# Decoder step on one core: two more feed-forward tiles by seven block products, sums moved between early tiles, and a regrouped norm of the last tokens

## What is computed

```python
x = x + g1 * rmsnorm(mixed, p['norm_post_mix'])
h2 = rmsnorm(x, p['norm_pre_ffn']) * (1 + sc2) + sh2
fg, fu = jnp.split(h2 @ p['w_ffn_in'], 2, axis=-1)        # 1024 -> 2 x 2816
ff = (jax.nn.silu(fg) * fu) @ p['w_ffn_out']              # 2816 -> 1024
x = x + g2 * rmsnorm(ff, p['norm_post_ffn'])
```

## Time and profile before

| | us |
|---|---|
| time, median of 3 runs (lowest to highest) | 1398.78 (1397.47 to 1404.78) |
| profiled execution: its time | 1403.48 |
| its span, first to last instruction | 1401.7 |
| PE busy in the span | 1352.4 (96%) |
| mean granted TensorE clock | 0.985 |

### The profile page before, as it was taken

How to read it: one execution, slowest core, us unless ns; L and a number is a source line. 1 busy time by engine, 2 the same in 40 slices (tenths; PEclk the granted TensorE clock), 3 DMA queues, 4 the chain that set the end, 5 groups by cost and what they waited for, 6 DMA issues and landing times.

```text
span 1401.7 us, 24171 instructions
## 1 busy us (share of the span) xinstructions
PE 1352.4 (96%) x10132; PEld 1256.8 (90%) x10132; DVE 793.5 (57%) x1110; ACT 555.8 (40%) x815; POOL 211.6 (15%) x320
## 2 busy tenths in 40 slices
PE   6899999999999999999999999999889999999996
PEld 3799999988997898799889978999789999999995
DVE  4459888522252484267437624874866788853224
ACT  4477778211222321232214123336543566542221
POOL 1122232000123222302320222000001111100001
PEclk8999999999999999999999999999999999999998
DMA  9422222582525334424442443336024676743323
GB/s 366 151 76 91 61 76 79 220 334 97 189 65 190 114 109 156 163 93 136 151 157 78 138 163 121 91 93 228 33 78 113 166 187 163 175 134 100 93 83 64
DMA packets 60267, 188.30 MB, mean 134 GB/s; under 512 B 6528, under 2 KB 9728, under 8 KB 59776
## 3 DMA queue, kind: packets, MB, share of 16 engines
q1 hardware_dynamic: 44096, 141.28, 29.7%
q0 software_dynamic: 14912, 43.39, 11.8%
q10 hardware_dynamic: 1152, 2.10, 0.4%
HBM read 163.19 MB, written 23.55 MB: 133 GB/s over the span
## 4 chain that ended last, share of the span: by engine, by line
PE 84%; DVE 9%; ACT 3%; issue 2%; DMA 1%; POOL 0%; SPq 0%; DVEq 0%; ACTq 0%; POOLq 0%
PE ps L893 56%; PE ps L1294 12%; PE ps L902 3%; PE ps L1142 2%; PE ps L1153 2%; PE ps L945 1%; PE ps L1125 1%; PE ps L1185 1%; PE ps L1171 1%; PE ps L1028 1%; DVE w_lo L1781 1%; ACT w_hi L1369 1%; PE ps L1082 1%; PE ps L1095 0%; DVE hs L1898 0%
## 5 line engine op out<-in xcount | busy, mean ns | idle before, releaser
L893 PE MATMUL ps<-h_hi,w_hi 128*128 128x272 f32 x1584 | 336.7, 294 | 7.6 <-DVE h_lo L1800 5.8
L893 PE MATMUL ps<-h_hi,w_lo 128*128 128x272 f32 x1584 | 329.6, 290 | 0.0
L893 PE MATMUL ps<-h_lo,w_hi 128*128 128x272 f32 x1584 | 328.6, 289 | 0.0
L1781 DVE TENSOR_TENSOR w_lo<-raw,w_hi 128x1024 fp32r<-128x1024 f32 (+2 forms) x158 | 187.1, 1188 | 218.3 <-ACT w_hi L1369 216.4
L893 PEld LDWEIGHTS ps<-h_hi,w_hi 128*128 128x128 f32 x1584 | 252.4, 190 | 20.9 <-issue 12.2
L1369 ACT ACTIVATE w_hi<-raw 128x1024 fp32r<-128x1024 f32 (+2 forms) x158 | 161.8, 1025 | 255.7 <-PE ps L893 150.3
L893 PEld LDWEIGHTS ps<-h_lo,w_hi 128*128 128x128 f32 x1584 | 250.8, 190 | 0.0
L893 PEld LDWEIGHTS ps<-h_hi,w_lo 128*128 128x128 f32 x1584 | 249.4, 190 | 0.0
L2058 DVE SCALAR_TENSOR_TENSOR state<-state,ps 128x512 f32<-128x512 f32 x64 | 41.1, 683 | 108.4 <-PE ps L1185 108.2
L2446 POOL DMA_DIRECT2D s_raw<-in_w_fin x16 | 13.8, 866 | 337.0 <-DMA s_raw<-in_w_fin 337.0
L893 PE MATMUL ps<-a_hi,w_hi 128*128 128x272 f32 x308 | 63.8, 288 | 0.3 <-DVE w_lo L1781 0.3
(11 more groups left out here) (291 smaller groups left out, 2634.3 us busy)
## 6 DMA issues: line engine op xcount, KB each, us to landing
raw<-in_w_head SPq DMA_DIRECT2D x48, 512.0 KB, 3.8
state<-in_state POOLq DMA_DIRECT2D x32, 512.0 KB, 4.5
out_rs<-state POOLq DMA_DIRECT2D x32, 512.0 KB, 4.5
raw<-in_w_rnn SPq DMA_DIRECT2D x24, 512.0 KB, 3.6
ada_more<-in_w_ada SPq DMA_DIRECT2D x23, 512.0 KB, 8.2
raw<-in_w_fin SPq DMA_DIRECT2D x22, 512.0 KB, 4.7
ada_raw<-in_w_ada SPq DMA_DIRECT2D x16, 512.0 KB, 14.8
raw<-in_w_bret SPq DMA_DIRECT2D x16, 512.0 KB, 3.5
```

The lines of the kernel that those rows point to most:

```text
L893: mm = nc.tensor.matmul(dst[:, half, :], a, b[:, half * HALF:(half + 1) * HALF], start=first and j == 0, stop=last and j == 2)
L1781: V.tensor_tensor(lo[:, 0:cols], raw_slab(i)[0][:, 0:cols], hi[:, 0:cols].bitcast(F32), ALU.subtract).then_inc(lo_ready, 1)
```

## The change

`FIRST` goes from 6 to 4: only n = 3 is a plain tile, 18 instead of 16 n's are made by block products. The sums of h2 and their splits move from the plain tiles to between the `product_half`s of the second early half. In `second_input(1)` the samples' operations move behind the second scaled tile, one of them ahead of the reciprocal; `silu_half(1, 0)` goes ahead of the root. For the first pair, DVE multiplies the last plain tile before it splits the third weight slab. At the end, PE adds the last tile's squares in PSUM (two matmuls with the ones) instead of DVE's addition; the samples are normed together with the last 160 prompt tokens, in three pieces of 3, 3 and 2 channel tiles, each stored by one DMA; the sum of squares of the first part stands after 4 blocks instead of 8 of the second part; and ACT takes a root of one element after the first output tile.

```diff
-FIRST = 6
+LAST_TILES = (slice(0, 3), slice(3, 6), slice(6, KD))
+FIRST = 4
...
-            for k in range(KD):
-                sp.wait_ge(y_done, k + 1)
-                sp.dma_start(out["y"][:, k, cols], xr_[:, k, cols]).then_inc(stored, 16)
+            for i, ks in enumerate(LAST_TILES):
+                sp.wait_ge(y_done, i + 1)
+                sp.dma_start(out["y"][:, ks, cols], xr_[:, ks, cols]).then_inc(stored, 16)
...
+                        if half and (i, j) == (0, 3):
+                            total_part(("post2", 0), LAST_PARTS[0], 3)
-                    if half and i == 0:
-                        total_part(("post2", 0), LAST_PARTS[0], 3)
-            total_part(("post2", 1), LAST_PARTS[1], 4)
+            pe.wait_ge(sq_added, 2 * KD - 2)
+            nc.tensor.matmul(dst, ccol("ones"), rsn[:, cols], start=True, stop=False)
+            pe.wait_ge(sq_ready, SQUARES)
+            nc.tensor.matmul(dst, ccol("ones"), sqn[:, (KD - 1) % 2, cols], start=False, stop=True).then_inc(full, 1)
...
+            silu_half(1, 0)
             std(("pre2",), 1, rsn, D, eps_rms)
-            silu_half(1, 0)
...
-            ahead(("fg", EARLY))
-            for n in range(EARLY):
-                silu_half(n, 1)
-            keep(1)
+            plain_ahead(("fg", EARLY))
+            silu_half(0, 1)
+            keep(1)
+            act.wait_ge(x1_stored, 16)
+            hi_of_sum(0)
+            hi_of_sum(1)
+            silu_half(1, 1)
+            hi_of_sum(2)
+            hi_of_sum(3)
+            silu_half(2, 1)
...
+                if m == 0:
+                    do(A(sqn[:, 1, 0:1], eps_rms[:, 0:1], ACT.Sqrt), wait=False)
...
+            hs2 = mo[:, :, SEQ:T]
+            do(V.tensor_tensor(all_samples(mo), all_samples(xr_), for_samples(scale2), ALU.mult))
+            product_half(1, 0)
             one_over("pre2", 1)
-            product_half(1, 0)
-            second_input(1)
+            second_input(1, samples_of_second)
...
+            plain_ahead(("fg", EARLY))
+            product_half(0, 1)
+            sums_of_input()
+            product_half(1, 1)
+            lo_of_sum(0)
+            lo_of_sum(1)
+            product_half(2, 1)
+            lo_of_sum(2)
+            lo_of_sum(3)
...
-            add_to_norm(first + KD + 1, KD - 1, LAST_PARTS[1], norm_summed)
             wait_took(dve, ("fo", KD - 1))
+            do(V.tensor_tensor(all_samples(mo), all_samples(mo), for_samples(gate2), ALU.mult))
             dve.wait_ge(xres_in, 32)
             one_over_last(1)
-            samples_normed(gate2)
-            for k in range(KD):
-                add_last(k)
+            for ks in LAST_TILES:
+                add_last(ks)
```

More of the change, by code:

```diff
@@ L1673, in _, with hi_of_sum @@
             silu_half(2, 0)
-            ahead(("fg", EARLY))
-            for n in range(EARLY):
-                silu_half(n, 1)
-            keep(1)
             def plain_ahead(key):
                 split_to(min(pl.slab[(*key, "w", 0)] + AHEAD, last_plain))
+            def hi_of_sum(i):
+                act.wait_ge(x_summed, i + 1)
+                name = ("XC", "XB", "XA", "XD")[i]
+                do(A(x_block(None, x_hi, name), x_block(None, mo, name), ACT.Copy), x_hi_ready, wait=False)
+            plain_ahead(("fg", EARLY))
[8 more added lines that the diff above has]
+            silu_half(2, 1)
             def hi_of_blocks(p, slab):
@@ L1720, in _ @@
                 plain_ahead(("fg", n))
[L1721 to L1725, removed]
                 act.wait_ge(a_ready, EARLY + n - 1 if n >= EARLY + 2 else n + 2)
@@ L2145, in samples_normed, with second_input @@
                 do(V.tensor_tensor(x, x, y, ALU.add))
-            def second_input(half):
+            def second_input(half, between=None):
                 at = prompt_of(half)
@@ L2153, in second_input @@
                                                   ALU.mult), h_scaled, wait=False)
+                    if between is not None and k == 1:
+                        between()
                     if k:
@@ L2191, in _, with samples_of_second @@
                     product_half(0, 0)
+            hs2 = mo[:, :, SEQ:T]
+            do(V.tensor_tensor(all_samples(mo), all_samples(xr_), for_samples(scale2), ALU.mult))
+            product_half(1, 0)
             one_over("pre2", 1)
-            product_half(1, 0)
[L2194 to L2199, removed]
-            second_input(1)
+            def samples_of_second():
+                do(V.tensor_tensor(hs2, hs2, rsn[:, SEQ:T].unsqueeze(1).to_broadcast([P, KD, NS]), ALU.mult))
+                do(V.tensor_tensor(all_samples(mo), all_samples(mo), for_samples(mod[:, 3 * KD:4 * KD, :]), ALU.add))
+                do(V.tensor_copy(h_hi[:, :, SEQ:T], hs2))
+                do(V.tensor_tensor(h_lo[:, :, SEQ:T], hs2, h_hi[:, :, SEQ:T].bitcast(F32), ALU.subtract))
+            second_input(1, samples_of_second)
             product_half(2, 0)
-            ahead(("fg", EARLY))
-            for n in range(EARLY):
-                product_half(n, 1)
             def plain_ahead(key):
@@ L2286, in _ @@
                     gated_pair(p - 1)
-                else:
-                    plain_gated(FIRST - 1)
                 lo_of_blocks(p, 3)
@@ L2291, in _ @@
                     lo_of_gated(p - 1)
+                else:
+                    plain_split(FIRST - 1)
                 if p + 1 < PAIRS:
@@ L2309, in norm_first, with add_last @@
                 do(V.tensor_tensor(y, y, rsn[:, LAST_PARTS[0]], ALU.mult), y_normed, wait=False)
[L2311 to L2313 removed]
+            def add_last(ks):
+                at = LAST_PARTS[1]
+                y, x = mo[:, ks, at], xr_[:, ks, at]
+                r = rsn[:, at].unsqueeze(1).to_broadcast([P, ks.stop - ks.start, at.stop - at.start])
                 do(V.tensor_tensor(y, y, r, ALU.mult))
```

39 lines of the change are left out of this document (23 added, 16 removed).

## The result

The changed kernel takes **1390.25 us** (median of 7 runs, 1389.64 to 1395.01) beside 1398.78 of the kernel before (7 runs, 1397.11 to 1404.78). The ratio is 0.9936, with a 95% interval from 0.9917 to 0.9955: 9.0 us faster, between 6.3 and 11.6. The forecast was 1388.0, with a range of 1384.5 to 1393.0.

A forecast was written before the change was run, and what follows sets the result against it. PE, busy 1352.4 of 1401.7 us, was taken to bound the kernel, with the end behind its last matmul. Terms of 3.0, 3.2, 2.8 and 1.8 sum to 10.8 us, off the median 1398.78: 1388.0 us, range 1384.5 to 1393.0.

The forecast's parts named there:

- two more tiles by products: Feed-forward input: two n's by block products save 24 matmuls of 0.125 us, 3.0 us, if a pair stays PE's.
- first pair: First block pair: product ahead of third slab's split removes PE's 1.8 us wait and a slow stretch of 1.4; 3.2 us.
- second early half: Second early half: first `h_lo` 1.8 us earlier, 1.0 us wait for `product_half(0, 1)` gone; 2.8 us, bounds 1.0 and 3.2.
- the end: Program's end: accumulations start 1.3 us earlier, stores without holes give 0.5; 1.8 us, bounds nothing and 3.6.
- holes between the stores: Program's end: DVE's late data left gaps among the last stores; their removal counted as 0.5 us.
- the two queues run side by side: Program's end: stores' packets should lie behind the accumulations'; stores and accumulations side by side would prove the prediction wrong.
- just fits: Second early half: product of `(2, 0)` frees its banks at 1029.2, PE asks at 1029.3, so no wait.
- The stores land on their own: Rival, program's end: accumulations don't hold stores back, gain there 3.6 us instead of 1.8, 1386.2 us; chance 0.08.
- The sums come late: Rival, second early half: `keep`, sums or splits 2.5 us later, 2 to 4 us less gain, 1391 us; chance 0.14.
- the first pair still waits: Rival, first block pair: PE waits for the third slab instead, 3.2 us less gain, 1391.2 us; chance 0.08.
- A pair stayed PE's: Block pairs: DVE's 8.5 us fit in PE's 10.5; rival that DVE sets the pace, 1406 us, chance 0.03.
- the third slab: Second early half: weight slab whose late load delayed `product_half(0, 1)`; no longer asked for there, 1.0 us.

The follow-up runs named there:

- e6: Changed kernel with FIRST = 6, and only two slabs of the plain tiles split ahead of the second half's first gate; 1393.17 us, 0.9958 of before.
- t2: Changed kernel with POOL's four last DMAs as plain writes, the addition of x to the first 352 tokens left out; 1387.27 us, 0.9914 of before.
- t3: Changed kernel with half of the accumulations replaced by DVE additions and SP stores, final POOL wait moved to SP; 1386.45 us, 0.9910 of before.
- s1: Changed kernel with the end of before, except the first part's sum behind four blocks and the root's table loaded early; 1390.39 us, 0.9933 of before.
- b1: Changed kernel plus a one-element Silu on ACT behind the second early half's root, loading the table early; 1389.58 us, 0.9927 of before.
- b2: Changed kernel with both half of the accumulations taken away (t3) and the Silu table loaded early (b1); 1386.18 us, 0.9904 of before.
- e4: Changed kernel, but DVE splits the first pair's third slab before the last plain tile's gated product, as before; 1391.80 us, 0.9941 of before.
- e5: Changed kernel with the sums of h and their splits moved back behind the early halves, FIRST still 4; 1397.29 us, 0.9986 of before.
- e3: Changed kernel with FIRST = 6 again, everything else as changed; 1397.14 us, 0.9980 of before.
- t1: Changed kernel, but SP instead of POOL waits at the end for the four accumulating DMAs; 1390.34 us, 0.9940 of before.

## Why the prediction held, and which term was off

| step | forecast us | measured us | from |
|---|---|---|---|
| two more tiles by products | 3.0 | 3.0 | FF of e6 and of the changed kernel |
| first pair | 3.2 | 3.6 | block matmuls of e6 and of before |
| second early half | 2.8 | 3.2 | reciprocal to first plain matmul, 28.0 and 24.8 |
| first early half | not in the sum | -0.9 | its 96 matmuls, 13.98 and 14.87 |
| the end | 1.8 | 0.9 | mean of the profiles; 0.5 in the profiled pair |

The terms measured add up to 9.8, the forecast was 10.8, and the timed runs give 9.0 (6.3 to 11.6). That the sum came so near is in part luck: two terms were 0.4 too small, against 0.9 too much at the end and 0.9 that no term had.

**The end is the term that was mis-sized**, 1.8 us forecast and 0.9 measured. Its mechanism was right in the main: the accumulations bind (t2 and t3), and DVE's 4.6 us don't count (s1). Counted from the last block matmul, the first part's reciprocal (1383.61 before, 1369.33 after) starts 1.5 us earlier, and so does the first accumulating packet (forecast 1.3). Three things went otherwise. The forecast had 0.5 us for holes between the stores, but s1, with the old stores, ends no later. The last accumulating packet ends only 0.7 us earlier in the profiled pair (0.9 on average): the stores' first packet comes 3.2 us ahead of that end, before it came 1.2 us ahead. So the two queues run side by side for longer, which the forecast named as a sign of being wrong; that this is what stretches the accumulations is likely, but no run shows it alone. And the forecast ended the program with the last store, when POOL's drain behind the accumulations ends later: in the changed kernel it lasts 2.48 us, in before 2.24.

**The second early half** took its upper bound of 3.2: 2.0 and 1.0 us of waits and the slow stretch behind the shorter wait (0.9 by b1 and b2) went, the new wait of 0.6 came. No run undoes the new order there alone, so this size is read from the two chains. In the changed kernel's profile the first half has a slow stretch twice as long, and 0.9 us went back there. Nothing in the change touches that wait, and in t2, whose code is the changed kernel's up to the last DMAs, the first half takes 13.9 us and the second has no slow stretch either; b1 and b2, too, show that where it falls differs between profiles of nearly the same code. The 0.6 us wait for `(2, 0)` was the place that "just fits": the gate ended as worked out (12.0 us behind the reciprocal's start; forecast 12.1), but PE, not slowed, came early.

**The first pair** was right in its wait (1.8) and in its owner; that the slow stretch goes with the wait holds between before and e6, but e4 had the wait and no slow stretch. Why is open.

**The rivals.** "The stores land on their own" falls with t2 and t3. "The sums come late" and "the first pair still waits" didn't happen; e4 prices a wait in the first pair at 2.0 us of FF, and e5, with the sums later still than that rival had them, loses 7.0. A pair stayed PE's: 189.38/18 = 10.5 us. The forecast treated the third slab as worth 1.0 us; e3 shows that with the sums moved behind it, it would have been 3.8.

## What to carry to other kernels

Where a load's wait stands ahead of work in an engine's order, price it by all that is queued behind: the third slab cost 1.0 us in one order and 3.8 in another, with the same load. At a kernel's end, look at which bytes hold the DMA engines before making the arithmetic faster: ending DVE 2.9 us earlier (the changed kernel beside s1) gave nothing that shows, taking half of the accumulations away and moving POOL's wait gave 2.8 us. A wait of a few us costs PE a slow stretch only sometimes, and in which stage it falls varies: compare stages over several profiles before giving it to an edit.

## What was not expected of the hardware

- POOL's drain at the program's end takes 2.2 to 2.5 us behind its last wait, and 9.1 to 11.7 us where it starts before its DMAs have landed (t1, t3, b2). There it ends 1.9 us behind the last landing, 2.7 us in the changed kernel. It was 2.48 in kernels with 18 pairs and 2.23 in those with 16; whether the count of POOL's DMAs makes that difference wasn't tried.
- Accumulating 1.44 MB takes 10.0 us of the 16 DMA engines, writing them 3.9, a factor of 2.6 (the forecast of t2 had 2.3). Packets of 1408 bytes in t3 take 152 and 62 ns, a factor of 2.5.
- The table load for Silu took 1.28 us, and the gate started 0.01 us behind it.
